# A hybrid attention and MLP decoder layer on one core: a start in small pieces and an end ordered by token tile

## The reference, cut to what matters

```python
n = rmsnorm(h, attn_norm_w)
proj = n @ w_in                        # 2048 x 2624
y_mla = mla_attention(...)             # 8 heads, rotary key, causal
y_nsa = nsa_attention(...)             # 16 heads, three branches with gates
y = concat([rmsnorm(y_mla), rmsnorm(y_nsa)])
h = h + y @ w_o                        # 2048 x 2048
n = rmsnorm(h, mlp_norm_w)
h = h + square(relu(n @ w_up)) @ w_down   # 2048 x 8192, 8192 x 2048
out = rmsnorm(h, final_norm_w)
```

## Time and profile before

| | us |
|---|---|
| median of 3 runs | 1116.69 |
| lowest, highest | 1115.11, 1116.77 |
| the profiled execution, its own time | 1115.32 |
| its span, first to last instruction | 1113.5 |
| PE busy | 1075.1 (97%) |
| DVE busy | 635.0 (57%) |
| ACT busy | 495.5 (44%) |
| POOL busy | 93.8 (8%) |
| HBM read | 187.82 MB, a mean of 171 GB/s |

### The profile page before, as it was taken

The page is one execution under the profiler, slowest core; times in us unless marked ns, Lnnn a source line. Parts: engine busy times, 40 slices in busy tenths (PEclk is TensorE's granted clock), DMA queues, the critical chain, the costliest instruction groups (busy, mean ns, idle before and its releaser), DMA issues.

```text
span 1113.5 us, 14179 instructions
## 1 busy us (share of the span) xinstructions
PE 1075.1 (97%) x5544; PEld 895.9 (80%) x5544; DVE 635.0 (57%) x769; ACT 495.5 (44%) x599; POOL 93.8 (8%) x157
## 2 busy tenths in 40 slices
PE   5999899999999999999999999999999999999995
PEld 4889787777777888888888888888888888888783
DVE  3654855677674655446545555554555554654664
ACT  3655444666664364334433433433433433433432
POOL 2134100323123000000000000000000000000002
PEclk9999999899999999999999999999999999999998
DMA  8476562142224556566566565565565565555541
GB/s 299 153 206 201 167 227 83 69 151 77 76 77 135 168 173 195 178 189 196 183 194 191 183 196 186 188 196 183 193 190 185 194 188 188 189 188 189 188 151 76
DMA packets 81807, 190.41 MB, mean 171 GB/s; under 512 B 8598, under 2 KB 20972, under 8 KB 81388
## 3 DMA queue, kind: packets, MB, share of 16 engines
q1 hardware_dynamic: 81772, 189.93, 53.1%
HBM read 187.82 MB, written 2.10 MB: 171 GB/s over the span
## 4 chain that ended last, share of the span: by engine, by line
PE 91%; DVE 4%; ACT 2%; issue 1%; DMA 1%; DVEq 0%; SPq 0%; POOL 0%; ACTq 0%
PE ps L1443 21%; PE ps L1103 17%; PE ps L1104 16%; PE ps L1107 16%; PE ps L1445 11%; PE ps L1308 2%; DVE w_lo L732 2%; PE ps L1282 1%; ACT w_hi L509 1%; PE ps L1258 1%; PE ps L1309 1%; PE ps L1261 1%; PE ps L1257 1%; PE ps L1405 1%; PE ps L1262 1%
## 5 line engine op out<-in xcount | busy, mean ns | idle before, releaser
L732 DVE TENSOR_TENSOR w_lo<-raw,w_hi 128x2048 fp32r<-128x2048 f32 (+3 forms) x197 | 405.6, 2062 | 371.4 <-ACT w_hi L516 295.1
L516 ACT ACTIVATE w_hi<-raw 128x2048 fp32r<-128x2048 f32 x120 | 230.2, 1919 | 398.1 <-PE ps L1107 200.4
L1443 PE MATMUL ps<-xT,w_hi 128*128 128x512 f32 x1024 | 361.9, 398 | 1.3 <-DVE h_sb L912 1.0
L1445 PE MATMUL ps<-xT,w_lo 128*128 128x256 f32 x1024 | 287.4, 281 | 0.0
L1443 PEld LDWEIGHTS ps<-xT,w_hi 128*128 128x128 f32 x1024 | 192.3, 188 | 49.0 <-issue 1.3
L1103 PE MATMUL ps<-w_hi,hidT 128*128 128x512 f32 x512 | 199.5, 390 | 2.4 <-issue 2.1
L1104 PE MATMUL ps<-w_lo,hidT 128*128 128x512 f32 x512 | 199.4, 389 | 0.0
L1445 PEld LDWEIGHTS ps<-xT,w_lo 128*128 128x128 f32 x1024 | 193.4, 189 | 0.5
L1107 PE MATMUL ps<-w_hi,hidT 128*128 128x512 f32 x512 | 157.7, 389 | 0.0
L509 ACT ACTIVATE w_hi<-raw 128x1024 fp32r<-128x1024 f32 (+3 forms) x77 | 107.1, 1397 | 84.5 <-PE ps L1107 61.6
L1103 PEld LDWEIGHTS ps<-w_hi,hidT 128*128 128x128 f32 x512 | 96.1, 188 | 23.3 <-issue 2.4
(11 more groups left out here) (250 smaller groups left out, 1031.0 us busy)
## 6 DMA issues: line engine op xcount, KB each, us to landing
raw<-in_w_up SPq DMA_DIRECT2D x64, 1024.0 KB, 5.2
raw<-in_w_down SPq DMA_DIRECT2D x64, 1024.0 KB, 5.4
raw<-in_w_o SPq DMA_DIRECT2D x16, 1024.0 KB, 5.4
raw<-in_w_in SPq DMA_DIRECT2D x8, 1024.0 KB, 5.0
raw<-in_w_in SPq DMA_DIRECT2D x8, 832.0 KB, 7.4
raw<-in_w_in SPq DMA_DIRECT2D x8, 816.0 KB, 4.3
raw<-in_mla_w_uq SPq DMA_DIRECT2D x12, 256.0 KB, 4.1
x_sb<-in_x SPq DMA_DIRECT2D x4, 512.0 KB, 7.1
```

The costliest lines, as they stand in the source:

```text
L516: act.activation(w_hi[:, j % SPLIT, :], raw[:, j % RAW, :], ACT.Copy).then_inc(hi_done, 1)
L732: return dve.tensor_tensor(dst, src, high.bitcast(F32), ALU.subtract)
L1443: pe.matmul(ps[:, b0 + f, :].rearrange("p (c t) -> p c t", c=2), w_hi[:, slot, w], xT[:, :, k0 + b, :], start=start and b == 0, stop=False)
L1445: m = pe.matmul(ps[:, b0 + f, 0:T], w_lo[:, slot, w], xT[:, 0, k0 + b, :], start=False, stop=stop and b == 3)
```

## The change

1. **Start.** x comes in five column ranges instead of two: columns 0 to 255 through ACT's queue, 256 to 511, and then three of 512, each right behind chunks 0, 1, 2 and 3 on SP's queue. Chunk 0 comes as two transfers, one for each of its blocks of 128 rows, and is split and multiplied block by block, with semaphores of their own. Ahead of the products PE runs 16 transposes of the identity matrix whose result nobody reads (`keep_warm`): 8 before x, 8 after the first two turned blocks.
2. **The norm of x.** Its sums of squares move from chunks 3 and 4 to chunks 5 and 6 on ACT, and DVE's part of the root from chunk 5 to chunk 7.
3. **Last group.** The loops on ACT and DVE run one group less, and the last group is written out. In it the activations are split at j = 13 and 14 into a buffer of their own (`hidZ`, over `xT`, which is free after j = 11); the split after the loop is gone, and the last down projection reads `hidZ`.
4. **Last chunk.** Chunk j = 7 after the loop is split into a place of its own (`w_end`, over the unused part of `yT`), so its split no longer waits for PE.
5. **End by token tile.** j = 6 and 7 are multiplied tile by tile: all of t = 0 first, then t = 1 in two halves of 512 columns. Residual sums, squares, root, scaling and stores follow for each tile by itself, in pieces of 1024 or 512 columns. POOL also takes columns 1024 to 1535 of t = 0 (two operations). There are six stores, one on ACT's queue.

```diff
@@ SP
-            for t in range(TT):
-                sp.dma_start(x_sb[:, t, 0:D // 2], x_rows[t][:, 0:D // 2]).then_inc(x_in[0], 16)
+            def load_x(q):
+                for t in range(TT):
+                    part = slice(512 * q if q else 256, 512 * q + 512)
+                    sp.dma_start(x_sb[:, t, part], x_rows[t][:, part]).then_inc(x_in[q], 16)
...
+                if c == 0:
+                    for k, landed in enumerate((head_in, raw_in[raw_slot(0)])):
+                        sp.dma_start(dst[:, k, :], src[0][:, k, :]).then_inc(landed, 16)
...
-                if c == 0:
-                    for t in range(TT):
-                        sp.dma_start(x_sb[:, t, D // 2:D], x_rows[t][:, D // 2:D]).then_inc(x_in[1], 16)
+                if c <= 3:
+                    load_x(c)
...
+            sp.wait_ge(normed0, 1)
+            sp.dma_start(o_rows[0][:, 0:1024], h_sb[:, 0, 0:1024]).then_inc(stored, 16)
+            sp.wait_ge(last_w, 1)
+            sp.wait_ge(normed1, 1)
+            sp.dma_start(o_rows[0][:, 1024:D], h_sb[:, 0, 1024:D]).then_inc(stored, 16)
+            for q, (done, count) in enumerate(((normed0, 2), (normed1, 2), (normed1, 3))):
+                sp.wait_ge(done, count)
+                part = (slice(0, 512), slice(1024, 1536), slice(1536, D))[q]
+                sp.dma_start(o_rows[1][:, part], h_sb[:, 1, part]).then_inc(stored, 16)
@@ POOL
+            third = h_sb[:, 0, 1024:1536]
+            pool.wait_ge(fsq, 3)
+            link(pool.tensor_tensor(third, third, fw[:, 1024:1536], ALU.mult))
+            pool.wait_ge(root0, 1)
+            pool.tensor_scalar(third, third, rc[:, 0:1], None, ALU.mult).then_inc(last_w, 1)
@@ ACT
+            for t in range(TT):
+                act.dma_start(x_sb[:, t, 0:256], x_rows[t][:, 0:256]).then_inc(x_first, 16)
...
+            x_hi(0)
+            head_split_hi(0)
+            x_hi(1)
+            head_split_hi(1)
+            x_hi(2)
+            x_hi(3)
+            for c in range(1, 8):
+                split_hi(c)
+                if c > 1:
+                    x_hi(2 * c)
+                    x_hi(2 * c + 1)
+                if c in (5, 6):
+                    t = c - 5
...
+                    if last and j in (13, 14):
+                        for pair in (2 * j - 26, 2 * j - 25):
+                            last_hidden_hi(pair)
+
+            def last_hidden_hi(pair):
+                act.wait_ge(hid_ok, 2 * G - 1 + pair // 2)
+                act.wait_ge(w_used, LOOP0 - GC + 12 + GC * (G - 1))
+                act.activation(hidZ[:, 0, 2 * pair:2 * pair + 2, :], hid[:, 2 * pair:2 * pair + 2, :], ACT.Copy).then_inc(hd_hi, 1)
+
+            with act.Fori(1, G - 1) as g:
+                group_hi(g, False)
+            group_hi(G - 1, True)
-            for pair in range(4):
-                hidden_hi(pair, 2 * G - 1 + pair // 2, LOOP0 - GC + GC * G)
...
+            act.activation(w_end[:, 0, :], raw[:, 7 % RAW, :], ACT.Copy).then_inc(hi_done, 1)
             for t in range(TT):
+                act.wait_ge(added, t + 1)
+                square_sum(t, 0, 1024, 12 + 2 * t, t)
+            act.wait_ge(last_in, 1)
+            square_sum(0, 1024, D, 13, 2)
+            act.wait_ge(root0, 1)
+            act.wait_ge(weighted, 1)
+            act.activation(h_sb[:, 0, 0:1024], h_sb[:, 0, 0:1024], ACT.Copy, scale=rc[:, 0:1]).then_inc(normed0, 1)
+            act.wait_ge(last_in, 2)
+            square_sum(1, 1024, 1536, 15, 3)
+            act.wait_ge(last_in, 3)
+            square_sum(1, 1536, D, 10, 4)
+            act.wait_ge(root1, 1)
...
@@ DVE
+            for b in range(2):
+                x_lo(b)
+                dve.wait_ge(hi_done if b else head_hi, 1)
+                part = slice(CW * b, CW * b + CW)
+                low(w_lo[:, split_slot(0), part], raw[:, raw_slot(0), part], w_hi[:, split_slot(0), part])\
+                    .then_inc(lo_done if b else head_lo, 1)
+            x_lo(2)
+            x_lo(3)
+            for c in range(1, 8):
+                split_lo(c)
...
+                if c == 7:
                     dve.wait_ge(ssq_ok, 2)
...
+            low(w_end[:, 1, :], raw[:, 7 % RAW, :], w_end[:, 0, :]).then_inc(lo_done, 1)
...
+            dve.wait_ge(first_done, 8 + 2 * (G - 1) + 1)
+            last_add(0, 1024, D)
+            dve.wait_ge(fsq, 2)
+            link(dve.tensor_scalar(ssq[:, 12:13], ssq[:, 12:13], 1.0 / D, EPS, ALU.mult, ALU.add))
+            dve.wait_ge(fsq, 3)
+            root(0, ssq[:, 13:14], ssq[:, 12:13], root0)
+            dve.wait_ge(last_t, 1)
+            last_add(1, 1024, 1536)
+            dve.wait_ge(fw_in, 16)
+            dve.wait_ge(root0, 1)
+            dve.wait_ge(last_t, 2)
+            last_add(1, 1536, D)
...
+            last_norm(0, 1536, D)
...
+            dve.wait_ge(fsq, 5)
+            root(1, ssq[:, 10:11], ssq[:, 14:15], root1)
+            dve.wait_ge(root1, 1)
+            last_norm(1, 1024, 1536)
+            last_norm(1, 1536, D)
@@ PE
             pe.wait_ge(consts, 1)
-            pe.wait_ge(x_in[0], 16 * TT)
-            for k in range(3):
-                turn_x(k)
+            keep_warm(4)
             pe.wait_ge(prm0_in, 16)
             pe.transpose(bank(7, KT), prm0[:, :], ident[0:KT, 0:KT]).then_inc(prm_t, 1)
-            turn_x(3)
+            keep_warm(4)
+            for k in range(2):
+                turn_x(k)
+            keep_warm(8)
...
+            pe.wait_ge(head_hi, 1)
+            pe.wait_ge(xt_hi, 1)
+            head_products(0, 0, w_hi, True)
+            pe.wait_ge(xt_lo, 1)
+            head_products(0, 1, w_hi, False)
+            pe.wait_ge(head_lo, 1)
+            head_products(0, 0, w_lo, False)
+            for k in (2, 3):
+                turn_x(k)
+            pe.wait_ge(hi_done, 1)
+            pe.wait_ge(xt_lo, 2)
+            head_products(1, 0, w_hi, False)
+            head_products(1, 1, w_hi, False)
+            pe.wait_ge(lo_done, 1)
+            head_products(1, 0, w_lo, False).then_inc(w_used, 1)
...
+            for j in (6, 7):
+                pe.wait_ge(lo_done, LOOP0 - GC + j + 1 + GC * G)
+                for n0 in (0, 512):
+                    m = last_block(0, j, n0)
+            m.then_inc(first_done, 1)
+            for n0 in (0, 512):
+                for j in (6, 7):
+                    m = last_block(1, j, n0)
+                m.then_inc(last_t, 1)
```

More of the change, by code:

```diff
@@ L362, in _ @@
             sp.dma_start(fw[:, :], a["final_norm_w"].rearrange("(o d) -> o d", o=1).broadcast_to((P, D))).then_inc(fw_in, 16)
[L363 to L368 removed]
+            sp.wait_ge(normed0, 1)
[7 more added lines that the diff above has]
+                sp.dma_start(o_rows[1][:, part], h_sb[:, 1, part]).then_inc(stored, 16)
+            sp.wait_ge(stored, 16 * 6)
         @block.gpsimd
@@ L690, in _, with group_hi @@
             move_up(1, 4, LOOP0 - 1, None)
-            with act.Fori(1, G) as g:
+            def group_hi(g, last):
                 for j in range(1, GC + 1):
@@ new lines, in _ @@
+            act.wait_ge(weighted, 1)
[5 more added lines that the diff above has]
+            act.wait_ge(root1, 1)
+            act.wait_ge(weighted, 2)
+            for q in range(2):
+                part = slice(512 * q, 512 * q + 512)
+                act.activation(h_sb[:, 1, part], h_sb[:, 1, part], ACT.Copy, scale=rc[:, 1:2]).then_inc(normed0, 1)
@@ L1025, in _, with group_lo @@
             add_up(1, 4, 2)
-            with dve.Fori(1, G) as g:
+            def group_lo(g, last):
                 for j in range(1, GC + 1):
@@ L1036, in _, with last_hidden_lo @@
                         add_down(0, 5 + 2 * g, LOOP0 - GC + 7 + GC * g, 4 * g)
+                    if last and j in (13, 14):
+                        for pair in (2 * j - 26, 2 * j - 25):
+                            last_hidden_lo(pair)
                 add_down(1, 6 + 2 * g, LOOP0 - GC + 15 + GC * g, 4 * g)
-            for pair in range(4):
-                hidden_lo(pair, 4 * G - 4 + pair)
+            def last_hidden_lo(pair):
+                dve.wait_ge(hd_hi, 4 * G - 3 + pair)
+                low(hidZ[:, 1, 2 * pair:2 * pair + 2, :], hid[:, 2 * pair:2 * pair + 2, :], hidZ[:, 0, 2 * pair:2 * pair + 2, :])\
+                    .then_inc(hd_lo, 1)
+            with dve.Fori(1, G - 1) as g:
+                group_lo(g, False)
+            group_lo(G - 1, True)
             END = LOOP0 + GC * (G - 1)
@@ new lines, in _, with last_add, root @@
+            dve.wait_ge(hi_done, END + 8)
+            low(w_end[:, 1, :], raw[:, 7 % RAW, :], w_end[:, 0, :]).then_inc(lo_done, 1)
+            def last_add(t, c0, c1):
+                o = h_sb[:, t, c0:c1]
+                b0 = 2048 + 1024 * t - 1024
+                dve.scalar_tensor_tensor(out=o, in0=flat[:, b0 + c0:b0 + c1], scalar=r1[:, t:t + 1], in1=o,
+                                         op0=ALU.mult, op1=ALU.add).then_inc(last_in, 1)
+            def root(t, part, rest, done):
```

(10 more changed lines are left out.)

139 lines of the change are left out of this document (67 added, 72 removed).

## The result

The changed kernel takes 1105.41 us (median of 4, 1105.02 to 1105.58), the kernel before, run beside it, 1116.12 (median of 4, 1115.11 to 1116.77): a ratio of 0.9909, 95% interval 0.9897 to 0.9920. The profiled executions are 1105.58 and 1115.32, their spans 1103.6 and 1113.5. Forecast were 1103.4 and a gain of 12.6 from span to span; it is 9.9.

A forecast was written before the change was run, and what follows sets the result against it. PE, carrying 91% of the chain of waits, was taken as the bound. Start 5.9, root of x -0.1 and tail 6.8 (last group and chunk included) gave 12.6, so 1102.7 or 1104.1, middle 1103.4 us; range 1100 to 1108.5.

The forecast's parts named there:

- rival D: Gap before the last down projection stays, held by something other than the split of `hid`: gain 10.5, 1105.5 us; chance 0.03.
- parts 4 and 5: Last group: PE's gap before the last down projection goes, gain 2.05; last chunk: no wait for its split, gain 0.45.
- Part 1: Start: PE's first product at 7.1 instead of 14.0, chunk 1 at 14.6 instead of 20.53; gain 5.9 us.
- Rival B: Quicker start: queue's rate dip goes, transposes raise the clock before the first product; gain 14.5, 1101.5 us; chance 0.15.
- The clock at the start: Chunk 0 on PE: some 1.5 us of its 6.5 are due to the low clock, 1.2 instead of 2.4 GHz.
- Part 2: SP's queue: five more DMAs delay chunk 4's issue from 15.2 to 18.8, still in time; cost 0, at most 0.5.
- Rival E: Slower: SP's queue starves PE, chunk 4 landing later than 25.9; turns the result beyond 40.7 (1119); chance 0.02.
- rival A: Start: small pieces are slow, chunk 1 lands at 14.5, PE starts it at 18.0; gain 9.2, 1106.8 us; chance 0.17.
- Part 3: Root of x, moved later on DVE: PE loses 0.5 before chunk 8, waits 0.4 less at chunk 10; cost 0.1.
- Part 6: Tail after PE's products: work and stores by token tile end at 1106.7 against 1113.5; 6.8, including 2.05 and 0.45.
- C: New wait in the tail or last group, from late `w_lo` or POOL holding SP's stores: gain 9.6, 1106.5; chance 0.10.
- F: Change does not do what it says, and stores bound the tail: within 2.2 us of before; chance 0.01.

The follow-up runs named there:

- a2: The changed kernel with the activations `hid` split after the loop again, as before the change; 1107.65 us.
- a4: The changed kernel with ACT and DVE splitting chunk 1 before they take turned blocks 2 and 3 of x; 1101.49 us.
- a1: The changed kernel with the start of the kernel before, the place of x's root included; 1109.62 us.
- b1: The changed kernel without the last eight idle transposes, those after the first two turned blocks; 1104.71 us.
- b2: The changed kernel without all sixteen idle transposes and the two `keep_warm(4)`; 1104.74 us.
- b4: The changed kernel with DVE's operations for x's root after chunk 6 instead of chunk 7; 1105.52 us.
- a3: The changed kernel with last chunk, order of PE's work, residuals, roots and stores as before the change; 1107.93 us.
- b3: The changed kernel with DVE alone scaling the last 1024 columns of token tile 0, without POOL; 1104.47 us.
- d1: The changed kernel with 16 more idle transposes in PE's two waits ahead of the 32 narrow matmuls; 1102.53 us.

## Why the prediction was right, and where it was off

The time of 1105.41 lies inside the range, and the likeliest case was the one that came: each stretch moved in the direction given, and the three places where PE stood still were the right ones. The time alone would not say so, since rival D had 1105.5, nearer than the forecast's 1103.4; what rules D out is the gap, which is gone after and back in a2. The sum was 2.7 us too large. Two terms were too large, by 1.3 (the start, at the sums) and 1.7 (the tail), the parts 4 and 5 together were 0.5 too small, and the middle lost 0.2. One sign that the prediction itself had named as wrong came true: over 5 us from the last product to the last store's issue. The last batch of stores begins 5.69 us after PE's end. And the first product, at 8.49, is outside its 6 to 8.

- **Part 1, the first product, was off by 1.4 us.** "x's first columns ... can be in at 4.5" was the step: they landed at 6.0. By 6 us the queues had moved 1.08 MB by the row above, and not the 0.6 that the step wanted for the 262 KB of x: their second half, issued at 1.18 on ACT's queue, took 4.8. Everything up to chunk 1 is late by that: product 8.49 instead of 7.1, chunk 1's start 16.03 instead of 14.6, with the wait in between as forecast (1.51 against "about 1.6"). Its cause was as argued, too: ACT's turned blocks stood ahead of the split, and a4 takes the wait away. The size of 5.9 comes out as 4.53 at the sums and 4.29 by a1.
- **The idle transposes** were costed at nothing, to end by 7 when the first split does. They ended at 8.83, since x came late, and held the first product up by 0.47 (b1). Their gain was put between 0 and 1.5 us, most of it hidden by chunk 1's readiness. b1 and b2 do not settle the size. Little would be hidden, though: chunk 1's split waits for the blocks turned after the first products (12.35 in b1, 11.21 after), so slow first products delay it as well. Rival B's "clock up before the first product" did not come true in any run.
- **The clock at the start** was read off durations (0.63 against 0.40 for 512 columns), and rightly. The view of the granted clock prints 1.00 there, but the trace's entries of the clock, from which it is made, begin only at 17.38 in the kernel before, with a rise to 1.0; ahead of the first entry it prints 1.00 for want of one. PE's starts, before, change their spacing at that entry, from 0.43 for 512 columns to 0.24:
```profile
16.70 0.63 PE L1104 MATMUL ps<-w_lo,xT 128*128 128x512 f32 x1
17.13 0.43 PE L1103 MATMUL ps<-w_hi,xT 128*128 128x320 f32 x1
...
17.91 0.40 PE L1103 MATMUL ps<-w_hi,xT 128*128 128x512 f32 x1
18.15 0.40 PE L1104 MATMUL ps<-w_lo,xT 128*128 128x512 f32 x1
```
- **Part 2** held: chunk 4 was issued at 15.41, ahead of the 18.8 forecast (two issues of x took 0.91 to 1.55 us, one of weights 0.44 to 0.49), and PE waited for none of chunks 2 to 7. Rival E is out. So is rival A: chunk 1 landed at 9.8, and the rates of 317 to 408 GB/s at 4 to 8 us are above those of rows 4. The Trainium skill (DMA: Bandwidth & Descriptors, section Bandwidth) would have had the small pieces lose; here chunk 1 landed 6.7 us after its issue, against 10.6 before, and 0.8 us earlier than forecast, so the 6 us that the prediction worked out from the page did not appear. The case is milder than "three extra pieces": six transfers stood ahead of it on the queues beside the norm weights, against five before, with fewer bytes.
- **Part 3** held: the forecast cost was 0.1, and 155.44 against 155.48 from sums to narrow leaves 0.04. b4 shows the exchange of one wait for the other.
- **Parts 4 and 5** held: 2.05 and 0.45 forecast, 2.21 by a2 and 0.60 by a3 found. DVE's split of j = 14 ended at 1037.8, with no wait behind it. The two make 2.81 of the 3.03 us; the rest is not assigned.
- **Part 6, the tail, was off by 1.7 us**, 2.62 against 4.3. The step "t = 0 is complete" and ACT's squares were right to 0.1. "I add half" for POOL holding DVE was not: the root's first operation took 0.92 in place of 0.16, and by b3 the whole of POOL's share costs 0.68. The Trainium skill's rule of full exclusion (SBUF — State Buffer, section Who interferes with whom), by which the root would wait the full 1.2, is the nearer one: the root came 0.38 us after POOL's operation had begun, waited for all that was left of it, 0.76 us, and ended 0.01 us after it. The last 1.05 MB were issued 5.69 us after PE's end instead of 4.75: 0.26 of that is POOL's hold beyond the half, 0.46 the handover from ACT's squares (read out at 1090.02) to the root's first operation at 1090.48, which had been given no time, and the rest small excesses of the pieces. The bytes then ran at 346 to 410 GB/s and not at 400, so that from the issue to the end it took 4.96 and not 4.15.
- **Rivals C and D.** Of C, a new wait in the tail, POOL's 0.68 came true, a quarter of its 3 us. B is out as well: it wanted 7.5 at the start, and 4.5 came. D is out by a2, F by the time.
- The middle was costed at 0, and it moved by -0.24. Most of that is the clock, below: it fell 0.1 us behind the first narrow matmul and not 0.3, and the 32 took 6.97 and not 6.79.

## What to carry to other kernels

When a start is opened up by splitting its first transfer, look at the order on the splitting engines next: here the second chunk had landed 2.6 us before ACT took it, behind work that was not ready yet. Price operations of a serial tail piece by piece, fixed parts included, and keep GpSimd off the SBUF while VectorE runs a chain of short operations. Look for waits of TensorE ahead of a run of narrow matmuls: in d1, filling two of them with idle transposes went with 2.9 us less, as much as the change's own reordering of the tail. And measure how far a stretch moves between kernels that do the same there before reading a small edit from one run.
